# A two-layer hybrid encoder trunk: norms one tile ahead, tail sums on TensorE, and a narrow opening gram

## The reference

```python
for layer in range(DEPTH):
    hn = rmsnorm(x, norm_mix[layer])
    if layer % 2 == 0:
        p = hn @ ab_w_in[j]        # then rwkv7_mixer and rglru_mixer on its columns
        x = x + jnp.concatenate([ya, yb], axis=-1) @ ab_w_out[j]
    else:
        x = x + hgrn2_mixer(hn, ...)
    hn = rmsnorm(x, norm_ffn[layer])
    x = x + hier_moe(hn, ...)      # each token: 2 of 32 experts, weighted by its two gates
return rmsnorm(x, norm_final)
```

## Time and profile before

| | us |
|---|---|
| median of 3 runs (lowest, highest) | 2823.05 (2820.83, 2830.72) |
| the profiled execution | 2824.96 |
| its span, first to last instruction | 2823.2 |
| TensorE busy in the span | 2550.8 (90%) |
| VectorE busy | 1927.1 (68%) |
| ScalarE busy | 1608.2 (57%) |

### The profile page before, as it was taken

One profiled execution on the slowest core, in us unless ns is written; L12 is line 12 of the kernel. 1 busy time (PEld: TensorE's weight loads), 2 busy tenths in 40 slices (PEclk: granted clock), 3 DMA queues, 4 the chain that ended last, 5 costly groups with the idle time before them and its releaser, 6 DMA issues. The chain is left out here.

```text
span 2823.2 us, 57974 instructions
## 1 busy us (share of the span) xinstructions
PE 2550.8 (90%) x20884; PEld 2081.7 (74%) x20884; DVE 1927.1 (68%) x2201; ACT 1608.2 (57%) x1874; POOL 395.3 (14%) x342
## 2 busy tenths in 40 slices
PE   5998889988979999999859999998797999999990
PEld 4776789956858888888748777776684888888870
DVE  3348356534379999999666666666436899999974
ACT  3655232344138888888635555555213788888861
POOL 0020000000003333333210000000000233333320
PEclk9999999988989999999969999999897999999995
DMA  3111000013259999999651111111324999999964
GB/s 97 46 38 38 27 4 4 4 61 114 76 191 361 378 385 384 381 377 377 227 194 31 34 36 33 37 31 46 122 76 151 359 377 378 382 384 385 382 245 189
DMA packets 219991, 525.39 MB, mean 186 GB/s; under 512 B 43824, under 2 KB 99120, under 8 KB 219824
## 3 DMA queue, kind: packets, MB, share of 16 engines
q1 hardware_dynamic: 201392, 489.34, 46.8%
q0 software_dynamic: 18432, 33.60, 3.1%
HBM read 506.06 MB, written 50.33 MB: 197 GB/s over the span
## 5 line engine op out<-in xcount | busy, mean ns | idle before, releaser
L1773 DVE TENSOR_TENSOR w_low<-w_raw,w_high 128x1024 fp32r<-128x1024 f32 x768 | 894.7, 1220 | 31.1 <-DVEq L52 21.4
L1473 ACT CAST w_high<-w_raw 128x1024 fp32r<-128x1024 f32 x768 | 755.4, 1050 | 107.5 <-ACTq L52 107.5
L1633 PE MATMUL ps<-w_high,x_high 128*128 128x512 f32 x1024 | 415.1, 405 | 7.6 <-PEq L52 6.7
L1637 PE MATMUL ps<-w_high,x_low 128*128 128x512 f32 x1024 | 404.1, 395 | 0.0
L1636 PE MATMUL ps<-w_low,x_high 128*128 128x512 f32 x1024 | 402.1, 393 | 0.0
L1633 PEld LDWEIGHTS ps<-w_high,x_high 128*128 128x128 f32 x1024 | 195.5, 191 | 50.6 <-issue 14.0
L1637 PEld LDWEIGHTS ps<-w_high,x_low 128*128 128x128 f32 x1024 | 194.3, 190 | 43.4
L1636 PEld LDWEIGHTS ps<-w_low,x_high 128*128 128x128 f32 x1024 | 195.1, 190 | 37.7
L1633 PE MATMUL ps<-w_high,hidden_high 128*128 128x512 f32 x512 | 200.8, 392 | 6.7 <-PEq L52 6.7
L1636 PE MATMUL ps<-w_low,hidden_high 128*128 128x512 f32 x512 | 200.5, 392 | 0.0
L1637 PE MATMUL ps<-w_high,hidden_low 128*128 128x512 f32 x512 | 200.4, 391 | 0.0
(11 more groups left out here) (421 smaller groups left out, 4928.0 us busy)
## 6 DMA issues: line engine op xcount, KB each, us to landing
w_raw<-in_moe_w_gate SPq DMA_DIRECT2D x256, 512.0 KB, 5.3
w_raw<-in_moe_w_up SPq DMA_DIRECT2D x256, 512.0 KB, 5.7
w_raw<-in_moe_w_down SPq DMA_DIRECT2D x256, 512.0 KB
w_raw<-expert_rows SPq DMA_DIRECT2D x32, 512.0 KB, 9.8
w_tiles<-in_c_w_in SPq DMA_DIRECT2D x28, 512.0 KB, 4.0
w_tiles<-in_ab_w_in SPq DMA_DIRECT2D x22, 512.0 KB, 3.9
residual<-in_x SPq DMA_DIRECT2D x16, 512.0 KB, 8.1
h_rows<-hn_moe SPq DMA_DIRECT2D x16, 512.0 KB, 2.9
```

The lines of the kernel that those rows point to most:

```text
L1473: act.copy(wh[:, p, :], raw[:, p, :]).then_inc(high_made, 1)
L1633: ins = pe.matmul(ps[:, bank, :], high, w_h, start=first, stop=False)
L1637: return pe.matmul(ps[:, bank, :], low, w_h, start=False, stop=final)
L1773: dve.tensor_tensor(wl[:, p, :], raw[:, p, :], wh[:, p, :].bitcast(F32), ALU.subtract).then_inc(low_made, 1)
```

## The change

It has five parts. (1) In the opening, the square and the root of tile t+1 are written ahead of the cast of tile t, and so are `rows` and `mean_square` on VectorE. (2) The tail of each MoE has the same order, two combines ahead. (3) In the first tail for tiles 0 to 3, in the last for all 8, TensorE makes the gate-weighted first row plus the residual in PSUM (`sum_rows`): a diagonal matrix of gates times the row, and the identity times the residual, 4 plain float32 matmuls of 128x512 a tile. VectorE then adds the second row in one instruction in place of two. One instruction makes the 8 diagonals (`row_scale`), ahead of the combines. (4) The squares go to a tensor of their own, and in the last tail `next_rows` has 8 slots, so that `next_square` waits for no DMA. (5) In HGRN2 the opening gram is made in 32 blocks of 32x32 around the diagonal in place of 8 of 128x128, and 12 matmuls of the projection move from ahead of the sum of squares to behind it.

```diff
@@ opening: ScalarE, VectorE
+                square(0)
                 for t in range(TT):
-                    square(t)
+                    if t + 1 < TT:
+                        square(t + 1)
+                    root(t)
                     if t:
                         high(t - 1)
-                    root(t)
...
+                mean_square(0)
                 for t in range(TT):
-                    mean_square(t)
+                    rows(t)
+                    if t + 1 < TT:
+                        mean_square(t + 1)
                     if t:
                         low(t - 1)
-                    rows(t)
@@ MoE tails: ScalarE
                 def next_square(t):
                     act.wait_ge(combined, t + 1)
-                    if t >= 2:
-                        if last_norm:
-                            act.wait_ge(rows_in[t % 2], 16 * (TT // 2 + t // 2))
-                        else:
-                            act.wait_ge(next_turned, t - 1)
...
+                next_square(0)
                 for t in range(TT):
-                    next_square(t)
+                    if t + 1 < TT:
+                        next_square(t + 1)
+                    next_root(t)
                     if t and not last_norm:
                         next_high(t - 1)
-                    next_root(t)
@@ TensorE
+                def sum_rows(t):
+                    if t == 0:
+                        pe.wait_ge(scales, 1)
+                    if t >= (4 if last_norm else 2):
+                        pe.wait_ge(used, 2 * (t - (4 if last_norm else 2)) + 2)
+                    take(pe, raw_in[2 * t % NPC], 16)
+                    for h in range(2):
+                        f = slice(h * HALF, (h + 1) * HALF)
+                        pe.matmul(ps[:, sum_bank(t) + h, :], scale_by[:, t, :], raw[:, 2 * t % NPC, f], start=True, stop=False)
+                        last = pe.matmul(ps[:, sum_bank(t) + h, :], c.ident[:], c.res[:, t, f], start=False, stop=True)
+                    last.then_inc(mixed, 1)
...
-                if not last_norm:
+                if last_norm:
                     for t in range(TT):
+                        sum_rows(t)
+                else:
+                    sum_rows(0)
+                    sum_rows(1)
+                    for t in range(TT):
+                        if t + 2 < summed_tiles:
+                            sum_rows(t + 2)
                         next_turn(t)
@@ VectorE
                 def combine(t):
+                    if t < summed_tiles:
+                        i, b = 2 * t + 1, sum_bank(t)
+                        take(dve, raw_in[i % NPC], 16)
+                        dve.wait_ge(mixed, t + 1)
+                        dve.scalar_tensor_tensor(out=c.res[:, t, :], in0=raw[:, i % NPC, :], scalar=gate[:, 1, t:t + 1],
+                                                 in1=ps[:, b:b + 2, :].rearrange("p b n -> p (b n)"), op0=ALU.mult, op1=ALU.add).then_inc(used, 2)
...
                 combine(0)
                 dve.wait_ge(next_in, 16)
+                combine(1)
+                next_mean(0)
                 for t in range(TT):
+                    next_rows(t)
+                    if t + 2 < TT:
+                        combine(t + 2)
                     if t + 1 < TT:
-                        combine(t + 1)
-                    next_mean(t)
+                        next_mean(t + 1)
                     if t and not last_norm:
                         next_low(t - 1)
-                    next_rows(t)
@@ HGRN2, TensorE
-                        for n in range(4):
-                            t = slice((4 * b + n) * P, (4 * b + n + 1) * P)
-                            last = pe.matmul(ps[:, 4 + b, n * P:(n + 1) * P], left[:, t], right[:, t], start=True, stop=True)
+                        for n in range(0, 4 * P, 32):
+                            t = slice(4 * b * P + n, 4 * b * P + n + 32)
+                            last = pe.matmul(ps[n % P:n % P + 32, 4 + b, n:n + 32], left[:, t], right[:, t], start=True, stop=True)
...
-                    project(8)
+                    project(4)
                     take(pe, s["sq_ready"])
...
-                    project(9)
+                    project(13)
```

More of the change, by code:

```diff
@@ L1222, in moe @@
             sem(n) for n in ("wo_high", "wo_low", "y_high", "y_low", "y_used", "projected", "added"))
-        res_in = [sem(f"res_in{t}") for t in range(TT)]
         next_in, combined, next_squared, next_var, next_std, next_ready, next_turned, high_done, low_done, kept = (
@@ L1260, in moe @@
              f32("cmp_over", NOV, NE), f32("over_expert", NOV), f32("turns_cmp", NOV // 2), f32("turns_f", 1),
-             *(f32(n, NBLK) for n in ("no_row", "place_f", "second"))])
+             *(f32(n, NBLK) for n in ("no_row", "place_f", "second"))],
+            [f32("out_rows", TT, D)])
         lay([f32("w_raw", NPC, D)],
@@ L1265, in moe @@
             [f32("at_pos", 2 * TT, P), f32("reach", 2 * TT, NBLK + 1), f32("at_block", 2 * TT, NBLK)],
-            [f32("next_rows", 2, D), f32("next_gain", D), *(f32(n, TT) for n in ("next_sums", "next_var", "next_std", "next_rstd"))])
+            [f32("next_rows", 2, D), f32("square_out", D), *(f32(n, TT) for n in ("next_sums", "next_var", "next_std", "next_rstd"))])
         lay([f32("hidden", FF), f32r("hidden_high", DN, P), f32r("hidden_low", DN, P)],
@@ L1272, in moe @@
              *(f32(n, TT, NG) for n in ("g_shift", "g_sel", "g_tmp"))])
[L1273 to L1274 removed]
+        lay([f32("y_rows", D)], [f32("gain_rows", D)], [f32("next_gain", D)])
+        lay([f32("x_rows", D)], [f32("row_scale", TT, P)])
+        xg, scale_by = at["x_rows"], at["row_scale"]
         gate = sb("gate_of", [P, 2, TT])
@@ L1297, in moe, with sum_bank @@
         hn2, gb2, ss2, var2, std2, rstd2 = (at[n] for n in ("next_rows", "next_gain", "next_sums", "next_var", "next_std", "next_rstd"))
+        if last_norm:
+            hn2 = at["out_rows"]
+        NB = TT if last_norm else 2
+        summed_tiles = TT if last_norm else TT // 2
+        def sum_bank(t):
+            return 2 * (t % 4) if last_norm else 4 + 2 * (t % 2)
         B_P, B_TR, B_L, B_R, B_S, B_T = 0, 5, 4, 5, 6, 7
@@ L1744, in add @@
                     if fetch is not None and h == 0:
-                        dve.wait_ge(res_in[t], 16)
+                        take(dve, res_in[t], 16)
                     r = c.res[:, t, h * HALF:(h + 1) * HALF]
@@ L1912, in next_rows @@
                     dve.wait_ge(next_std, t + 1)
+                    if t >= 2 and not last_norm:
+                        dve.wait_ge(next_turned, t - 1)
                     ch(dve.reciprocal(rstd2[:, t:t + 1], std2[:, t:t + 1]))
-                    dve.scalar_tensor_tensor(out=hn2[:, t % 2, :], in0=c.res[:, t, :], scalar=rstd2[:, t:t + 1], in1=gb2,
+                    dve.scalar_tensor_tensor(out=hn2[:, t % NB, :], in0=c.res[:, t, :], scalar=rstd2[:, t:t + 1], in1=gb2,
                                              op0=ALU.mult, op1=ALU.mult).then_inc(next_ready, 1)
```

15 lines of the change are left out of this document (11 added, 4 removed).

## The result

The changed kernel takes **2788.4 us** (median of 4 runs, 2785.0 to 2791.3), the kernel before 2822.5 beside it (2820.8 to 2830.7): ratio 0.9868, 95% interval 0.9852 to 0.9884. The direction was right, the size was half.

What follows compares the result with a forecast made beforehand. TensorE, busy 90% of the span, bounds the kernel, except in the opening and tails, where a ring of small steps through three engines does. -13.3+8.5-8.1-3.7 = -16.6 from 2824.96 gives 2808.4, expected median 2806, range 2796 to 2817.

Steps and rivals of the forecast that it cites:

- the walk of the first tail: First tail, queues stepped through with prices: first head at 1458.1 in place of 1449.6, so +8.5, bounds +4 and +11.
- per head 0.4+0.7 = 1.1, seven times: HGRN2: each head saves 0.4 by the narrow gram and 0.7 by the moved matmuls; with the last head's 0.4, -8.1.
- the walk of the opening: Opening, 8 tiles stepped through three queues: project(0, 1) at 49.1 in the new order, 62.4 in the old, so -13.3.
- The upper bound of 16: Opening: 16 saved if the denser transposes bring the matmuls of project(0, 0) to the faster spacing sooner.
- the lower bound: Opening: only 10 saved if the split weights of block 1, loaded once block 0's split frees the tile, become the wait.
- the sum of tile 3 stands behind the first turn ... and ends at about 1438: First tail: TensorE's sum for tile 3 is held by the first turn, which waits for late rows; ends at about 1438.
- the wrong row: HGRN2's opening gram: 64 records of 32x32 priced at 1.40, from 32 such records in 0.70, against 2.02 before.
- The hole: Last tail: the 10.1 in which the third square waits for an output DMA would go.
- the ring: Last tail: combine 1.3, square 1.2, root 0.2, reciprocal and rows 1.5 bind at 4.2 a tile.
- The rival of a slow clock: Both tails: sums stay at half clock, 6.8 each, making the total +7.2, so 2830; chance 0.06.
- the forecast's own case: Whole kernel: a time of 2800 to 2812, chance 0.62.
- the floor of about 25 ns: HGRN2's gram: by a skill rule matmuls start no closer, so 64 take 1.6 and the part saves 1.6 less.

Runs made afterwards that it cites:

- g2_warm_before: The kernel before plus idle matmuls in TensorE's waits of the opening, fewer than in f5_warm_before: 2812.2 us, ratio 0.9954.
- g3_best_warm: The changed kernel with the first tail as before, VectorE's second weight split behind the diagonal pick, and short idle matmuls in the opening's waits: 2787.8 us, ratio 0.9859.
- e1: The kernel before with the opening's part of the change alone: 2809.7 us, ratio 0.9946.
- e2: The kernel before with HGRN2's opening gram as 64 narrow products and nothing else: 2816.5 us, ratio 0.9967.
- e4: The kernel before with both MoE tails as in the change and nothing else: 2824.7 us, ratio 0.9999.
- f5_warm_before: The kernel before plus idle matmuls in TensorE's waits of the opening, order unchanged; they outlasted some waits: 2823.7 us, ratio 0.9998.
- g4_fewer: g3_best_warm with four idle matmuls fewer in the opening (8 instead of 10 behind turns 5 and 7): 2781.9 us in one run.

## Why the prediction was wrong, point by point

The steps that failed are these: TensorE's clock, which no term of the sum held, gave about 11 us; "per head 0.4+0.7 = 1.1, seven times" took one head at the upper clock for all seven; the walk of the first tail ran 4 us late; and the walk of the opening gave the order 13.3 where it is worth 10.9.

**The opening** (forecast -13.3, measured -16.9). The mechanism was right, and the size of the order alone was too large: with the clock held up in both orders (g2_warm_before, g3_best_warm), 63.6 becomes 52.7, which is -10.9. The other 6 are the clock. The old order loses 8.9 to it (72.5 - 63.6), the new one 3.0 (a mean of 55.7 over ten profiles - 52.7). The step that failed is "I take the difference of the walks, 13.3". Both walks used lengths read at whatever clock the old order had, 1.97 for the transposes among them, and let them stand in the new order. The upper bound of 16 named the right effect, "denser transposes", and gave it too little. The condition of the lower bound came true as well, without its price: project(1, 0) does wait for the split weights of block 1, 2.62, but for their place in the queues and not for a load.

**The first tail** (forecast +8.5, measured +4.5). The order does delay the first head, by 3.1; the 0.8 found for the sums lie within the scatter of 0.9. The first sum took 5.6, not 6.3. The step that failed is "the sum of tile 3 stands behind the first turn ... and ends at about 1438", 22.4 behind the arrival. It did stand there, but it was done by 19.5, and rows 3 followed it by 8.2 and not by 9.4, so they came 27.7 behind the arrival and not 31.8, and all behind it was 4 earlier.

**HGRN2** (forecast -8.1, of which 7.7 are in the measured stretch; measured -14.5). Without the lower clock a head goes from 63.1 (g2_warm_before) to 61.8 (the changed kernel): 441.8 to 432.3 is -9.5, 1.4 a head where 1.1 was forecast. So this part's working was nearly right. The gram was priced by the wrong row (32x32 in one order of strips; the row of 64 records in 0.74 was the nearer one), but as forecast the bank caps what it can give: narrow alone gave 0.5 to 1.0 in the heads at the upper clock. The remaining 5.0 are the three heads at the lower clock. The failed step is "per head 0.4+0.7 = 1.1, seven times": rows 8 show one head, at the upper clock, and three of the seven are not like it. The seven periods from gram to gram would have shown it: 63.1, 63.2, 64.7, 64.7, 64.7, 63.3, 63.0.

**The last tail** (forecast -3.7, measured -5.8). The hole went as forecast, though it was smaller than the forecast reads it: the 10.1 are ScalarE's idle time, and VectorE's combines were 11.6 apart there instead of 4.6, so it was worth 7.1. The walk of the new order did not use it. The first sum was 0.9 shorter and the ring 4.04 instead of 4.2.

**The sum.** Against the forecast the profiled pair is 19.6 us faster: opening 3.6, first tail 4.0, HGRN2 6.4, last tail 2.1, and 3.5 in unchanged stretches, which is chance. About 11 of the whole gain (6 in the opening, 5 in HGRN2) is TensorE's clock, which no term of the sum held. The rival of a slow clock was there, but for one place only, and with the wrong sign for this kernel: the change made TensorE's waits shorter, and the clock was up for longer (0.961 on average against 0.950). The chances were also too sure: the forecast's own case had 0.62, and no case stood for "more than forecast" beyond 8 us.

**Which wait lets the clock fall.** Waits ahead of the gram of 1.88: 3, 3, 2, 5, 2 and 0 of seven heads at the lower clock (before, e1, e2, e4, f5, g2; the two of f5 have a pause as well). Waits of at most 1.23: none in 12 profiles (84 heads); in g3 and g4 three of fourteen, each behind one of the pauses of 2.4 to 2.5; the pause of 1.9 had none. So in these profiles the fall stands behind a stretch of 1.9 or more without a matmul, and with the wait cut to 1.2 it is gone. But g2 shows that it need not fall even then, with the same code and waits. What decides between 5 and 0 heads isn't settled. The Trainium skill says in "TensorE: Matmul & The Clock Gate", section "What's actually happening", that the count of slow matmuls varies between runs of one kernel with where the chip's watching stands. The trace agrees that it varies, for the opening: 9 and 18 slow matmuls in two profiles of the changed kernel, 8 to 20 over the new order. Why it varies no run here shows.

## What to carry to other kernels

Before pricing a repeated stage from one of its turns, list the period of every turn and the granted clock of each: a turn that differs by 1.6 us is a term. Where an edit shortens TensorE's waits, or puts its work back to back, add what the matmuls behind the wait save at the upper clock, and where a wait can't be cut, idle matmuls in it may be worth more than the edit: 13 us here with fillers that nearly fit the waits, nothing that the times can tell with longer ones. They also move the instructions behind them, and with that a pause can come or go. When two versions differ by less than the executions do, compare their stages in the traces, not their times.

## What the runs showed that I had not expected

- The records of narrow matmuls, 32 columns by 32, start 12 ns apart on average when neighbouring products write different strips of 32 partitions, and 23 ns apart when they write the same strip (0.75 and 1.49 for 64). The Trainium skill, "TensorE: Matmul & The Clock Gate", section "Part 3: Packing small matmuls — row/col tiling", says that matmuls in different tiles of the array overlap. The trace agrees, and the floor of about 25 ns that the prediction weighed fits only the second order.
- Pauses of 0.8 to 2.5 in the middle of a gram, with no releaser in the trace, in f5_warm_before, g3_best_warm and g4_fewer and in no other profile. They stand at a fixed instruction (16 instructions fewer moved them by exactly 8 records of two instructions), and only in the two heads that the loop's branch back leads to. They cost about 1.6 us in the one head without the lower clock behind the pause and 3.6 to 3.9 in the five with it. The Trainium skill, "Runtime: NRT & Kernel Launch", section "Instruction fetch mechanics", says that instructions are fetched ahead in blocks and that a taken branch can make an engine wait for the fetch. The traces agree: blocks of 16 KB, two at each branch back, and every pause ends 1.25 to 1.41 behind the landing of the second. No run changed the fetch itself.
- The same code up to the first tail ended 8 us apart in two profiles of the changed kernel (1395.8 and 1403.8), 2.6 of which are there at 57 us already.
